# Weight tiles cut at their readers' bounds, the values' columns multiplied inside the mixers, rows read by GpSimd's queue, and the state-space tables moved behind the second input projection

## The reference

```
h = rmsnorm(x); qa,ka,va,iq,ik,iw,qb,kb,vb,gate = split(h @ w_in0)   # 6992 columns
q, k, iq, ik = rope(...)                       # va and vb are not roped
o_a = attention over the 64 keys of best index score; o_b = banded (dilated) attention
x = x + (concat(o_a, o_b) * silu(gate)) @ w_out0
h = rmsnorm(x); qc,kc,vc,qd,kd,vd,fl,gate = split(h @ w_in1)         # 8200 columns
o_c = stick-breaking attention(qc,kc,vc); o_d = forgetting attention(qd,kd,vd, log_sigmoid(fl+b_f))
x = x + (concat(o_c, o_d) * silu(gate)) @ w_out1
second block: proj = rmsnorm(x) @ w_in (gated delta rule, RWKV, state-space and gate columns),
three branches, a product with each one's weights, a gated sum, one more product, rmsnorm
```

## Time and profile before

| | us |
|---|---|
| median of 3 runs | 2708.78 (2703.81 to 2711.19) |
| profiled execution | 2711.58 |
| its span, first to last instruction | 2709.7 |
| PE busy in the span | 2402.2 |
| DVE busy | 1639.6 |
| ACT busy | 1081.0 |
| POOL busy | 105.2 |
| mean granted TensorE clock | 0.950 |

### The profile page before, as it was taken

One profiled execution on the slowest core, in us unless ns is written; L12 is line 12 of the kernel. 1 busy time (PEld: TensorE's weight loads), 2 busy tenths in 40 slices (PEclk: granted clock), 3 DMA queues, 4 the chain that ended last, 5 costly groups with the idle time before them and its releaser, 6 DMA issues. The chain is left out here.

```text
span 2709.7 us, 30747 instructions
## 1 busy us (share of the span) xinstructions
PE 2402.2 (89%) x11932; PEld 1980.3 (73%) x11932; DVE 1639.6 (61%) x2365; ACT 1081.0 (40%) x1471; POOL 105.2 (4%) x174
## 2 busy tenths in 40 slices
PE   6989486899999578999999889888999889889996
PEld 5777355788888477877777768676678778777875
DVE  4588567554444254667999675655945544547754
ACT  4433144444444364554333552223543222234443
POOL 0100000100000000000000100001010000010100
PEclk9999798999999789999999999998989999989998
DMA  6666522766666424857555733238683332257753
GB/s 209 211 234 237 211 86 73 254 210 210 212 220 217 177 81 141 328 183 254 181 179 168 244 123 108 78 111 327 225 296 110 111 96 90 78 193 262 251 184 112
DMA packets 224944, 492.68 MB, mean 182 GB/s; under 512 B 16080, under 2 KB 34480, under 8 KB 219680
## 3 DMA queue, kind: packets, MB, share of 16 engines
q1 hardware_dynamic: 204000, 390.09, 42.8%
q0 software_dynamic: 20800, 100.63, 10.2%
HBM read 428.22 MB, written 62.46 MB: 181 GB/s over the span
## 5 line engine op out<-in xcount | busy, mean ns | idle before, releaser
L156 DVE TENSOR_TENSOR mm_lo<-mm_raw,mm_hi 128x1024 fp32r<-128x1024 f32 (+4 forms) x664 | 791.5, 1198 | 546.4 <-ACT mm_hi L149 539.1
L149 ACT CAST mm_hi<-mm_raw 128x1024 fp32r<-128x1024 f32 (+4 forms) x664 | 680.7, 1029 | 934.0 <-PE mm_acc L239 902.8
L239 PE MATMUL mm_acc<-mm_hi,mm_aT_hi 128*128 128x512 f32 (+4 forms) x2176 | 886.6, 407 | 110.7 <-DVE mm_lo L156 71.8
L239 PE MATMUL mm_acc<-mm_hi,mm_aT_lo 128*128 128x512 f32 (+4 forms) x2176 | 855.7, 393 | 0.0
L239 PE MATMUL mm_acc<-mm_lo,mm_aT_hi 128*128 128x512 f32 (+4 forms) x2176 | 855.3, 393 | 0.0
L239 PEld LDWEIGHTS mm_acc<-mm_hi,mm_aT_hi 128*128 128x128 f32 x2176 | 424.2, 195 | 216.4 <-DVE mm_lo L156 81.7
L239 PEld LDWEIGHTS mm_acc<-mm_hi,mm_aT_lo 128*128 128x128 f32 x2176 | 421.5, 194 | 84.4
L239 PEld LDWEIGHTS mm_acc<-mm_lo,mm_aT_hi 128*128 128x128 f32 x2176 | 424.2, 195 | 74.3 <-issue 1.0
L201 ACT ACTIVATE mm_stage<-mm_acc,mm_row_scale 128x512 f32<-128x512 f32 (+4 forms) x124 | 77.0, 673 | 108.8 <-PE mm_acc L239 70.5
L239 PE MATMUL mm_acc<-mm_hi,in_yT_hi 128*128 128x512 f32 x256 | 102.3, 400 | 3.2 <-DVE mm_lo L156 3.2
L239 PE MATMUL mm_acc<-mm_hi,in_yT_lo 128*128 128x512 f32 x256 | 101.1, 395 | 0.0
(11 more groups left out here) (589 smaller groups left out, 2498.3 us busy)
## 6 DMA issues: line engine op xcount, KB each, us to landing
mm_raw<-in_w_in SPq DMA_DIRECT2D x456, 512.0 KB, 5.3
mm_raw<-in_w_out SPq DMA_DIRECT2D x96, 512.0 KB, 5.4
proj<-mm_stage SPq DMA_DIRECT2D x55, 512.0 KB, 3.1
mm_raw<-in_w_branch SPq DMA_DIRECT2D x48, 512.0 KB, 5.3
mm_raw<-in_w_in SPq DMA_DIRECT2D x32, 416.0 KB, 5.0
home_tab<-s5t_tab POOLq DMA_DIRECT2D x4, 2048.0 KB, 7.7
s_tab<-home_tab POOLq DMA_DIRECT2D x8, 1024.0 KB, 6.2
odd_pr<-proj SPq DMA_DIRECT2D x2, 3076.0 KB, 13.1
```

What stands on the lines that cost most here:

```text
L149: self.nc.scalar.copy(self.hi[:, c % RING, :, 0:t.w], self.raw[:, c % RAW, :, 0:t.w]).then_inc(self.hi_done, 1)
L156: self.nc.vector.tensor_tensor(self.lo[:, c % RING, :, 0:t.w], self.raw[:, c % RAW, :, 0:t.w], self.hi[:, c % RING, :, 0:t.w].bitcast(F32) ...
L239: last = nc.tensor.matmul(self.acc[s][m][:, 0:t.w], t.aT[a][:, k, m * P:(m + 1) * P], b[:, c % RING, k - k0, 0:t.w], start=(k == 0 and fir ...
```

## The change

- `w_in0` is cut into 9 tiles of 464 columns (all that rope and transposes read, up to `C_VB` = 4176), 2 of 384 (the values `vb`) and 4 of 512 (the gate): 15 tiles (120 chunks) in place of 14 (112) with the same columns. `w_in1` is cut into 10 tiles of 512 (up to `C_VD` = 5120), one of 416 that starts with the forget logits, 2 of 512 (the values `vd`) and 4 of gate (three of 416, one of 392): 17 tiles as before, in another order.
- A mixer starts when its turned columns are done; the values' tiles are multiplied inside it. `even_mix` and `odd_mix` have 40 chunks beside them in place of 24, and read the values in a DMA of their own (`v_in`), which PE waits for ahead of the softmax heads.
- The rows are read by GpSimd's queue and not by SP's. SP still reads the constants. `even_mix` waits for each half of the rows by itself, `odd_mix` for three groups of columns.
- In `even_mix` DVE moves 6 chunks on before it waits for rows, and rope has 12 pace points for 14 chunks; the further shares are 5, 4, 7 and 4. In `odd_mix` they are 8 before the first turn, 5 between the turns of the two attentions, 15 in the stick-breaking loop, 8 in the softmax and 4 at the end.
- `s5_tables` runs behind 9 tiles (72 chunks) of `w_in1` after `seam` "in1", no longer behind 7 of `w_in0`. `seam` "in0" now has 72 chunks of its own, `seam` "in1" 16 of `w_in1`.
- The tile that the seam after a mixer holds back is 512 columns wide in layer 0 (336 before), 392 in layer 1 as before.

```diff
 def even_mix(...):
-        n_rope, n_dots, n_top, n_end = n_all * 5 // 16, n_all // 4, n_all // 8, n_all // 6
-        rope_pace = Pace(mm, n_rope, 3 * MT)
+        n_load, n_rope, n_dots, n_top, n_end = 6, n_all // 2, n_all // 8, n_all // 10, n_all // 10
+        rope_pace = Pace(mm, n_rope - n_load, 3 * MT * 2)
...
             def _(sp):
                 mm.sp_out(sp)
-                mm.wait_stored(sp, needed)
-                for m in range(MT):
-                    sp.dma_start(pr[:, m, :], prv[:, m, 0:EVEN_MIX]).then_inc(x_in, 16)
...
             def _(pool):
+                mm.wait_stored(pool, needed)
+                for m in range(MT):
+                    pool.dma_start(pr[:, m, 0:C_VB], prv[:, m, 0:C_VB]).then_inc(x_in[m], 16)
+                mm.wait_stored(pool, values)
+                pool.dma_start(pr[:, :, C_VB:EVEN_MIX], prv[:, :, C_VB:EVEN_MIX]).then_inc(v_in, 16)
...
                 pe.wait_ge(chosen, 1)
+                pe.wait_ge(v_in, 16)
                 soft.tensor(pe, soft_pace)
...
-                dve.wait_ge(x_in, 16 * MT)
+                mm.dve(dve, n_load)
                 dve.wait_ge(const_in, 128)
                 for m in range(MT):
+                    dve.wait_ge(x_in[m], 16)
...
                         st.link(V.tensor_tensor(tv[3], a, sb_, ALU.mult))
+                        rope_pace.dve(dve)
                         V.tensor_tensor(a, tv[0], tv[1], ALU.subtract)
                         st.link(V.tensor_tensor(b, tv[2], tv[3], ALU.add))
                         rope_pace.dve(dve)
 def odd_mix(...):
-        n_turn, n_c, n_end = n_all // 8, n_all * 5 // 12, n_all // 6
+        n_turn, n_d, n_c, n_end = 8, 5, n_all * 3 // 8, n_all // 10
...
             def _(pool):
+                prv = proj.rearrange("(m p) n -> p m n", p=P)
+                mm.wait_stored(pool, needed)
+                for c0, c1, arrived in ((0, C_QD, c_in), (C_QD, C_VD, d_in), (C_FL, ODD_MIX, f_in)):
+                    pool.dma_start(pr[:, :, c0:c1], prv[:, :, c0:c1]).then_inc(arrived, 16)
+                mm.wait_stored(pool, values)
+                pool.dma_start(pr[:, :, C_VD:C_FL], prv[:, :, C_VD:C_FL]).then_inc(v_in, 16)
...
-                turner.turn(pe, jobs)
-                turner.all_copied(pe, len(jobs))
+                turner.turn(pe, jobs_c)
+                mm.pe(pe, n_d)
+                turner.turn(pe, jobs_d)
+                turner.all_copied(pe, len(jobs_c) + len(jobs_d))
...
                 mm.dve(dve, n_turn)
-                dve.wait_ge(x_in, 16 * MT)
+                for arrived, q, n, ticked in ((c_in, C_QC, N_C, n_d), (d_in, C_QD, N_D, 0)):
+                    dve.wait_ge(arrived, 16)
+                    c = pr[:, :, q:q + n * HD]
+                    st.tell(V.tensor_scalar(c, c, SC, None, ALU.mult), scaled)
+                    mm.dve(dve, ticked)
+                dve.wait_ge(f_in, 16)
                 dve.wait_ge(const_in, 128)
-                for m in range(MT):
-                    c = pr[:, m, C_QC:C_QC + N_C * HD]
-                    V.tensor_scalar(c, c, SC, None, ALU.mult)
-                    c = pr[:, m, C_QD:C_QD + N_D * HD]
-                    st.tell(V.tensor_scalar(c, c, SC, None, ALU.mult), scaled)
 def program(nc, a, out):
+        turned0, values0, gate0 = (mm.add(a["w_in0"], proj0, c, w) for c, w in (
+            ((0, C_VB), 464), ((C_VB, EVEN_MIX), 384), ((EVEN_MIX, EVEN_MIX + D), TN)))
...
+        turned1, forget1, values1, gate1 = (mm.add(a["w_in1"], proj1, c, w) for c, w in (
+            ((0, C_VD), TN), ((C_FL, C_FL + 416), 416), ((C_VD, C_FL), TN), ((C_FL + 416, ODD_MIX + D), 416)))
+        turned1 = turned1 + forget1
...
-        seam(nc, "in0", a, mm, x, in0[:3], in0[3:], norms=[a["norm0"]])
-        s5_tables(nc, "s5t", a, mm, in0[3:n0], ...)
-        even_mix(nc, "even", a, mm, in0[:n0], in0[n0:-1], proj0, y0)
-        seam(nc, "in1", a, mm, x, in1[:n1], in1[n1:], (y0, (proj0[:, EVEN_MIX:], in0[:-1]), in0[-1:], out0), [a["norm1"]])
-        odd_mix(nc, "odd", a, mm, in1[:n1], in1[n1:-1], proj1, a["b_f1"], y1)
+        held0, held1 = gate0[-1:], gate1[-1:]
+        behind0 = values0 + gate0[:-1]
+        seam(nc, "in0", a, mm, x, turned0, behind0 + held0, norms=[a["norm0"]])
+        even_mix(nc, "even", a, mm, turned0, values0, behind0, proj0, y0)
+        seam(nc, "in1", a, mm, x, turned1[:2], turned1[2:] + values1 + gate1,
+             (y0, (proj0[:, EVEN_MIX:], turned0 + behind0), held0, out0), [a["norm1"]])
+        s5_tables(nc, "s5t", a, mm, turned1[2:], ...)
+        odd_mix(nc, "odd", a, mm, turned1, values1, values1 + gate1[:-1], proj1, a["b_f1"], y1)
```

More of the change, by code:

```diff
@@ L747, with even_mix @@
 TAKEN = -3.0e38
-def even_mix(nc, name, C, mm, needed, behind, proj, y):
+def even_mix(nc, name, C, mm, needed, values, behind, proj, y):
     SC = float(HD) ** -0.5
@@ L775, in even_mix @@
         sel = ph.sb("sel", [P, MT, SEQ])
-        x_in, const_in, roped, dots_full, dots_relu, added, chosen, own_v, stored = (ph.sem(s) for s in (
-            "x_in", "const_in", "roped", "dots_full", "dots_relu", "added", "chosen", "own_v", "stored"))
+        x_in = [ph.sem(f"x_in{m}") for m in range(MT)]
+        v_in, const_in, roped, dots_full, dots_relu, added, chosen, own_v, stored = (ph.sem(s) for s in (
+            "v_in", "const_in", "roped", "dots_full", "dots_relu", "added", "chosen", "own_v", "stored"))
         prv = proj.rearrange("(m p) n -> p m n", p=P)
@@ L941, with odd_mix @@
 ODD_MIX = C_FL + N_D
-def odd_mix(nc, name, C, mm, needed, behind, proj, b_f, y):
+def odd_mix(nc, name, C, mm, needed, values, behind, proj, b_f, y):
     SC = float(HD) ** -0.5
@@ L1003, in _ @@
                 mm.sp_out(sp)
-                mm.wait_stored(sp, needed)
-                for m in range(MT):
-                    sp.dma_start(pr[:, m, :], proj.rearrange("(m p) n -> p m n", p=P)[:, m, 0:ODD_MIX]).then_inc(x_in, 16)
                 sp.dma_start(bf[:, :], bcast_rows(b_f)).then_inc(const_in, 16)
@@ L1084, in _ @@
                 mm.act(act, n_turn)
-                turner.copy(act, jobs)
+                turner.copy(act, jobs_c)
+                mm.act(act, n_d)
+                turner.copy(act, jobs_d)
                 act.wait_ge(pre, 1)
@@ L1119, in _ @@
                 mm.dve(dve, n_turn)
-                dve.wait_ge(x_in, 16 * MT)
-                dve.wait_ge(const_in, 128)
-                for m in range(MT):
-                    c = pr[:, m, C_QC:C_QC + N_C * HD]
-                    V.tensor_scalar(c, c, SC, None, ALU.mult)
-                    c = pr[:, m, C_QD:C_QD + N_D * HD]
-                    st.tell(V.tensor_scalar(c, c, SC, None, ALU.mult), scaled)
+                for arrived, q, n, ticked in ((c_in, C_QC, N_C, n_d), (d_in, C_QD, N_D, 0)):
[4 more added lines that the diff above has]
+                dve.wait_ge(f_in, 16)
+                dve.wait_ge(const_in, 128)
                 st.tell(V.tensor_tensor(lf[:, :, :], pr[:, :, C_FL:C_FL + N_D], bf[:, :].unsqueeze(1).broadcast_to([P, MT, N_D]), ALU.add), pre)
```

24 lines of the change are left out of this document (10 added, 14 removed).

## The result

| | before | after |
|---|---|---|
| median | 2709.99 (2703.81 to 2712.67, 4 runs) | 2685.51 (2682.11 to 2693.06, 4 runs) |
| ratio to before | | 0.9903, 95% interval 0.9883 to 0.9922 |
| profiled execution; its span | 2711.58; 2709.7 | 2693.06; 2691.3 |
| second profile of the same kernel (after_again, below) | | 2688.49; 2686.6 |

The kernel is 24.5 us faster; I said 55. The sign is right and the time lies inside the range, but the size is under half.

The account below looks back on a forecast made before the run. TensorE's matmul stream with holes (busy 2402 of 2710 us) was taken to bound the kernel. Terms summed to -55.6 from the profiled 2711.6, giving 2656, 2653 of the median, stated as 2655; own range 2640 to 2676, 8-in-10 range 2636 to 2688.

Parts of the forecast that it names:

- Meanwhile VectorE has done its 6 chunks and the 2 ahead: In even_mix before rope: chunk work on VectorE and TensorE covers the rows' landing at 15.5 us, until about 16.6.
- The constants lose their place behind the rows: In even_mix's rows stretch: constants no longer queue behind the rows and SP is not blocked; no cost was given.
- The half share: Both mixers' row loads: GpSimd gets half of 317 GB/s, some 4 us later each, sum -49; not adopted.
- the row of 10.3 us: Profile row of GpSimd's 2 MB load beside weight loads, taken as the landing time for even_mix's first half of rows.
- even rows and rope: even_mix up to its first turn: stretch about as long as before but holding 20 chunks, -25.7 us (-28 to -13).
- odd rows: odd_mix before its first turn: 1.0 us of hole in place of 20.3, -19.3 us; -12 with a late landing.
- tables: The tables' phase, moved from 56 chunks to 72: each hole shrinks by some 1.5 us, -5 in all (0 to -12).
- The loop: odd_mix's stick-breaking loop: 5 more chunks, stretch from 74.4 to 80 us, not stream 52 to 45, -7.0 us.
- The slow clock: Rival: TensorE stays at 1.2 GHz in the filled stretches, +18 us in rope and +10 in the loop: 2683; chance 0.1.
- The rows land late: Rival, both mixers: first row loads take about 24 us, so -25.7 becomes -13 and -19.3 becomes -12: 2674; chance 0.13.
- The one that ended slower: Rival, tables' phase: VectorE's own work and the stream run in series, +57 and +16 us: 2728; chance 0.05.
- "Wrong" signs: Signs against it: rows after 20 us, halves waiting on ScalarE, table holes over 4 us, weights holding ScalarE, seam waits.

Follow-up runs that it names:

- after_again: The changed kernel itself, unedited, timed once more on the same chip as the other runs: 2689.93 us, ratio to before 0.9913.
- e12: Changed kernel with VectorE moving 3 chunks on, not 6, before it waits for rows in even_mix, the other 3 at rope's pace points: 2686.31 us.
- e2: Changed kernel with both mixers' constants issued by GpSimd's queue, ahead of its wait for the stored projection: 2684.59 us.
- e6: As e2, with GpSimd filling the rows with 0.5 in place of loading them, all but eight columns of each group: 2669.99 us.
- e5: As e2, with GpSimd issuing the second part of the rows only when the first has landed, in both mixers: 2674.16 us.
- e10: Kernel before the change, with SP issuing the constants ahead of its wait for the projection and of the rows: 2713.07 us.
- e7: As e5, with four of the tables' 72 chunks taken from the pace points and put behind the last table: 2669.38 us.
- e1: Changed kernel with rows read in pieces of 464 columns (even) and 512 (odd), same queue and bytes: 2684.26 us, ratio 0.9887.
- e4: Changed kernel with the rows read by SP's queue again, behind the constants, the values still by GpSimd's: 2683.79 us.

## Why the prediction was wrong in size

**The step that failed** is "Meanwhile VectorE has done its 6 chunks and the 2 ahead, and TensorE has 8 chunks of 2.08 = 16.6 us: covered". I priced the rows' landing beside weights and took the weights' own landing for granted. The rows did land early (+12.9 and, in odd_mix, +15.6 from the phase's start, where I had 15.5 and 19.7). The ring holds five chunks at the phase's start; the sixth was issued 6.0 us in, behind eight constants, and landed at +20.4 with the rows. Since VectorE's order has the halves of eight chunks ahead of rope, rope began at +24.2, not +15.5. That is the first failed step. The second is that "The constants lose their place behind the rows", which I took to make them no term: the last one landed at +19.3, and e12 shows that rope would have waited for it with no half in the way. From there all went as worked out: in ten of eleven profiles with this order the stretch ended 42.6 to 42.9 us after rope began (43.8 in e2), and the sum had 42.7. So 8.7 us of the miss are that start. In odd_mix the same starvation is 13.4: 14.4 for 1.0. The two are 22 of the 37 us by which the profile misses the sum.

The experiments show the cause by taking it away in parts. Constants off SP's queue and the phase's first weights issued that much earlier (e2) give 4.5 and 5.9 us; with that, taking the transfer out gives another 3.2 and 4.4 (e6: 15.0 and 4.1, for my 14.0 and 1.0), and loading the rows in two steps 0.8 and 5.1 (e5). In e2 the constants land earlier and the weights are issued earlier at once; which of the two the 4.5 us of even_mix are is not shown.

**The half share.** I had set that rule aside for the row of 10.3 us. That row gave the rows' landing within 2 us (8.6) and said nothing of who loses. The loser was in the same view of before (490 to 545 us): weights took 8.0 us to land there, 5.4 over the whole kernel. (The row also gives 4.0 + 0.7 + 10.3 = 15.0 and not the 15.5 that I went on with, half a us of the even term.) The Trainium skill, "DMA: Bandwidth & Descriptors", "Queues, rings and completion order", says that each DMA engine goes round the queues that have work, a whole packet at a time; the trace agrees (103 against 105 packets). My reading of it, half the bandwidth each, did not follow, as the packets were 15 and 1 KB: it was 93 to 8 in time.

**Term by term**, against the first profile (us, change from before):

| term | predicted | measured |
|---|---|---|
| tiles (pitch of 464 columns 2.507, not 2.48) | +1.3 | +3.2 |
| seam "in0", seam "in1" with the held tile | +0.6 | +1.8, -1.0 |
| even rows and rope | -25.7 | -17.0 |
| even, turns to the end | -1.5 | +1.2 |
| odd rows | -19.3 | -5.9 |
| between the turns, loop, softmax | -6.0 | -8.0 |
| tables | -5.0 | +3.5; second profile -0.7 |
| seam "in2" and second block, unchanged | 0 | +3.8; second profile +2.4 |
| sum | -55.6 | -18.4 |

The pitch is seen where TensorE is full, four k-block starts apart (answers to the earlier trace rows): 2.51.

```profile
150.16 0.37 PE L239 MATMUL mm_acc<-mm_hi,mm_aT_hi 128*128 128x464 f32 x1
...
152.67 0.37 PE L239 MATMUL mm_acc<-mm_hi,mm_aT_hi 128*128 128x464 f32 x1
```

The part from seam "in2" on is the same in all kernels and varies from 1635.3 to 1642.2 us (in the kernel before 1636.6, in e10 1641.2), so the +3.8 is no effect of the change.

The loop was right: -6.1 for -7.0. Of its two steps with two chunks one took 9.05 us and one 9.58 (the copies of z at 926.98 and 936.56; answers to the earlier trace rows), for the 8.10 of one chunk and my 9.1; in the longer one the second half waits 0.45 for its rounding:

```profile
926.98 0.55 DVE L1156 COPY odd_z<-odd_lg_ps 128x384 f32<-128x384 f32 x1
...
934.15 1.02 DVE L156 TENSOR_TENSOR mm_lo<-mm_raw,mm_hi 128x832 fp32r<-128x832 f32 x1
935.62 1.02 DVE L156 TENSOR_TENSOR mm_lo<-mm_raw,mm_hi 128x832 fp32r<-128x832 f32 x1 [0.45 <-ACT mm_hi L149]
936.56 0.55 DVE L1156 COPY odd_z<-odd_lg_ps 128x384 f32<-128x384 f32 x1
```

**Tables.** The four holes did shrink, but by 1.6 us in sum and not 5: TensorE's waits at the tables' ends are 2.40, 2.40, 2.40 and 2.74 us, for 2.40, 2.69, 3.47 and 3.02 before. The phase's end cost 3.2 more: the last 2 MB store and the barrier are 8.35 us of TensorE's wait, for 5.15, a term that I had put at 0 because the store only moves from one mixer's entry to the other's; e7 takes that wait away. So two more terms failed here: holes sized at 1.5 each, and a move priced at nothing. The difference between the two profiles, 44.5 and 40.3, is nearly all the granted clock: TensorE is busy 208.65 and 205.01 us for the same 910 matmuls, at a mean clock of 0.95 and 0.97, and idle 27.9 and 27.3. It shows at the same hole in both (first after, then after_again):

```profile
714.90:719.90 5.00, 4.96 (x15) 3.94 (x16) 4.62 (x15) 0.63 (x1) 0.00 (x0) 0.66 1.04 404
```

```profile
714.30:719.30 5.00, 4.99 (x22) 4.14 (x23) 4.62 (x15) 1.05 (x1) 0.00 (x0) 1.00 1.07 413
```

15 matmuls in 5 us at a clock of 0.66, 22 at 1.00, after the same hole of 2.4 us. Why one hole is followed by the lower level in one execution and not in another stays open.

**The rivals.** The slow clock's 2683 is the figure nearest to the result, and that is luck: its mechanism did not occur, with a granted clock of 0.92 in the rope stretch, 0.68 before, and 0.88 in the loop, 0.82 before. "The rows land late" gave 2674, also for a reason that did not occur: rows were early, weights and constants were late. The forecast's own range ended at 2676; that the time lies inside the wider one rests on these two rivals and not on the forecast's mechanism. The one that ended slower, the lead in the tables' phase, fell: 44.5 and 40.3 not stream for the 90 it needed. "Wrong" signs had the true one in the list: weights as a releaser of ScalarE for more than a few us. I named it and gave it no price.

## What to carry to other kernels

When a large load is put beside a running stream, price the stream's own next loads, not only the large one: ask how many chunks are buffered, when the next is issued, and how many bytes stand ahead of it. Keep small loads (constants, the first weights of a phase) ahead of it: that gave 4.5 and 5.9 us here. Split it into parts that wait for one another if the first part is not itself what is waited for: that gave 5.1 us in odd_mix and 0.8 in even_mix. Which queue issues it made no difference here, and issuing it earlier, ahead of the phase's weights, lost 6.2 us in odd_mix. And an engine whose written order has stream work ahead of its own waits for the stream, even when its own data are there.

## What the hardware showed that I had not expected

- Two DMA queues with work took turns packet by packet: 103 and 105 packets, 1.57 and 0.11 MB in 4 us. With rows in narrow pieces (e1) it was 417 and 415 packets, and the bytes 1.52 and 0.82 MB in 6 us. Over windows that also hold constants and stretches with one queue alone the counts differ (475 and 654, 812 and 1609).
- On one queue alone (e4) weights issued behind rows waited just as long, 16.8 us.
- 2.1 MB took 8.6 us to land with SP's queue held down to 28 GB/s, and 12.4 us when issued behind constants and five weight loads of the phase (e2). The sum over both queues was 419 and 394 GB/s in the changed kernel (224 to 228 and 846 to 860 us), 365 with narrow rows (846 to 860) and 375 with all on SP's queue (e4, 221 to 234).
- 64 KB of constants issued beside 4.2 MB of rows took 13.8 us to land, 3.4 us ahead of them on the same queue (e4).
- After an equal hole TensorE was granted 0.66 or 1.00 over the next 5 us in two executions of one kernel; over the tables' phase TensorE was busy 208.65 or 205.01 us for the same matmuls.
